# Sixteen of the 29 row sets gathered behind the lead latent block's merge, gathered behind the branches of all latent blocks instead

## The reference, cut to what matters

```
# branches: z and the two halves of the gMLP come from the same normalised input h
o  = rmsnorm(o, dn_norm) * silu(z)                     # z = h @ w_z
vg = rmsnorm(gelu(h @ w_vg), gm_norm)
gm = gelu(h @ w_u) * (w_s @ vg + b_s)                  # mixes positions inside a block of 128
# merge
merged = sigmoid(h @ w_ga) * (o @ w_a) + sigmoid(h @ w_gb) * (gm @ w_b)
x = x + gt1 * (merged @ w_out)
# PEER, for each token: 8 heads x 16 experts = 128 experts out of 16384, each a row of 2048
act = gelu(sum_d h2[d] * peer_u[expert, d]) * gate     # 128 dot products
y   = sum over the 128 experts of act * peer_v[expert] # 128 weighted additions
```

## Time and profile before

| what | value |
|---|---|
| median of 3 runs | 5527.45 us (5520.8 to 5527.68) |
| the profiled execution | 5512.66 us, its span 5510.9 us |
| busy, share of the span | PE 55%, PEld 38%, DVE 70%, ACT 9%, POOL 54% |
| DMA | 1866.24 MB, mean 339 GB/s |
| gathers (L320), as GpSimd's instructions | 640 of `peer_u` and 640 of `peer_v` |
| VectorE's uses of row sets | L367 x640, mean 2323 ns; L372 x635, mean 2357 ns |

### The profile page before, as it was taken

The page is one execution under the profiler, slowest core; times in us unless marked ns, Lnnn a source line. Parts: engine busy times, 40 slices in busy tenths (PEclk is TensorE's granted clock), DMA queues, the critical chain, the costliest instruction groups (busy, mean ns, idle before and its releaser), DMA issues. The chain is left out here.

```text
span 5510.9 us, 40820 instructions
## 1 busy us (share of the span) xinstructions
PE 3046.0 (55%) x15606; PEld 2074.5 (38%) x15606; DVE 3874.0 (70%) x4382; ACT 510.0 (9%) x834; POOL 2982.5 (54%) x1524
## 2 busy tenths in 40 slices
PE   5989978998999997979998893000000000000000
PEld 2786955448995447665554352000000000000000
DVE  2340017986675763267774689999999999999998
ACT  1521002422221000000000000000000000000000
POOL 0131002754654642104453522888888888888886
PEclk7999989999999998989999997555555555555555
DMA  9819878982226979959998854999999999999998
GB/s 398 347 54 342 322 293 322 395 359 96 88 85 265 388 277 375 383 215 379 420 420 361 328 209 180 422 420 422 422 421 420 420 419 420 421 409 422 422 422 363
DMA packets 269191, 1866.24 MB, mean 339 GB/s; under 512 B 31362, under 2 KB 35714, under 8 KB 48836
## 3 DMA queue, kind: packets, MB, share of 16 engines
q0 software_dynamic: 194560, 1409.51, 62.6%
q1 hardware_dynamic: 67812, 414.04, 19.4%
q10 hardware_dynamic: 6624, 40.07, 1.8%
HBM read 1844.56 MB, written 18.94 MB: 338 GB/s over the span
## 5 line engine op out<-in xcount | busy, mean ns | idle before, releaser
L220 PE MATMUL ps<-arena_sb 128*128 128x128 f32 (+2 forms) x8704 | 1872.9, 377 | 121.5 <-PEq L1641 31.6
L320 POOL DMA_INDIRECT arena_sb<-peer_v,arena_sb x640 | 1337.7, 2090 | 762.9 <-DVE arena_sb L372 475.4
L372 DVE SCALAR_TENSOR_TENSOR arena_sb<-arena_sb 128x2048 f32<-128x2048 f32 x635 | 1497.0, 2357 | 176.0 <-DMA arena_sb<-peer_v,arena_sb 99.4
L367 DVE CUSTOM_DVE_ANT_0 arena_sb<-arena_sb 128x2048 f32<-128x2048 f32 x640 | 1478.7, 2323 | 176.2 <-DMA arena_sb<-peer_u,arena_sb 174.5
L320 POOL DMA_INDIRECT arena_sb<-peer_u,arena_sb x640 | 1255.5, 1962 | 548.9 <-issue 275.5
L220 PEld LDWEIGHTS ps<-arena_sb 128*128 128x128 f32 x8704 | 1261.0, 195 | 748.1 <-issue 431.2
L266 POOL DMA_DIRECT2D arena_sb<-w_mod x64 | 34.9, 545 | 610.1 <-PE ps L227 487.6
L842 POOL TENSOR_TENSOR arena_sb<-arena_sb 128x1024 f32<-128x1024 f32 x60 | 197.9, 3307 | 202.7 <-ACT arena_sb L1100 166.9
L1502 PE MATMUL ps<-arena_sb 128*128 128x512 f32 x640 | 279.6, 599 | 30.9 <-PEq L1355 30.7
L1420 DVE TENSOR_TENSOR arena_sb<-ps,arena_sb 128x128 f32<-128x128 f32 (+1 forms) x96 | 35.2, 378 | 344.1 <-PE ps L220 343.0
L912 PE MATMUL ps<-arena_sb 128*128 128x64 f32 x1760 | 208.6, 277 | 0.0
(11 more groups left out here) (224 smaller groups left out, 2268.3 us busy)
## 6 DMA issues: line engine op xcount, KB each, us to landing
arena_sb<-w_mod POOLq DMA_DIRECT2D x64, 1024.0 KB, 8.8
arena_sb<-w_qkv SPq DMA_DIRECT2D x48, 1024.0 KB, 8.8
arena_sb<-w_ga SPq DMA_DIRECT2D x48, 1024.0 KB
arena_sb<-w_gb SPq DMA_DIRECT2D x48, 1024.0 KB
arena_sb<-w_out SPq DMA_DIRECT2D x48, 1024.0 KB, 7.5
arena_sb<-w_query SPq DMA_DIRECT2D x48, 1024.0 KB, 8.0
arena_sb<-w_mod SPq DMA_DIRECT2D x32, 1024.0 KB, 10.1
arena_sb<-w_a SPq DMA_DIRECT2D x48, 512.0 KB, 7.9
```

Of the source, the lines that this page charges most:

```text
L220: mm = pe.matmul(out, weights[:, k * P:(k + 1) * P], x[:, k, :], start=(k == 0), stop=(k == chunks - 1))
L320: nc.gpsimd.indirect_dma_start(slot, None, a["peer_v" if adds else "peer_u"], bass.IndirectOffsetOnAxis(ap=g.index[:, p:p + 1], axis=0)).t ...
L367: nc.vector.tensor_tensor_reduce(rows, rows, total, 1.0, 0.0, ALU.mult, ALU.add, g.dots[:, p:p + 1]).then_inc(t.rows_used, 1)
L372: nc.vector.scalar_tensor_tensor(out=total, in0=rows, scalar=g.weight[:, p:p + 1], in1=total, op0=ALU.mult, op1=ALU.add).then_inc(t.rows_u ...
```

## The change

It moves numbers in two lists. In the latent `branches` the eight z steps get 5, 4, 5, 4, 5, 4, 5, 4 row sets instead of 4 each, the run ahead of the norm of vg 40 instead of 34, and the first six u steps 5 instead of 4 (the seventh keeps 4, the eighth none): 4 + 6 + 6 = 16 more, 110 instead of 94. In the lead block's `merge` the steps get one set each for the first 13 and none for the last three, instead of two for 14 and one for the fifteenth: 13 instead of 29. From the end of that merge on, every set has the number, the slot and the place that it had.

```diff
@@ -1139,7 +1139,7 @@ def branches(nc, t, a, g):
     m0 = 3 * H
-    behind = take(t, [0] * (2 * H + 1) if ctx else [4] * H + [34] + [4] * (H - 1) + [0], 4)
+    behind = take(t, [0] * (2 * H + 1) if ctx else [5, 4] * (H // 2) + [40] + [5] * (H - 2) + [4, 0], 4)
     z_behind, vg_behind, u_behind = behind[0:H], behind[H], behind[H + 1:]
@@ -1348,7 +1348,7 @@ def merge(nc, t, a, g):
     sets = 1 if ctx else 2
-    behind = take(t, [0] * KD if ctx else [2] * (KD - 2) + [1, 0] if nb == 1 else [10] * (KD - 2) + [4, 0], 5)
+    behind = take(t, [0] * KD if ctx else [1] * (KD - 3) + [0, 0, 0] if nb == 1 else [10] * (KD - 2) + [4, 0], 5)
     m0 = 5 * H
```

## The result

The changed kernel takes 5536.73 us (median of 18 runs), the kernel before 5520.1 (18 runs): ratio 1.0026, interval 1.0019 to 1.0034. The medians differ by 16.6 us, the ratio says 14: slower, where 7.5 us faster was forecast. One run of the changed kernel, 5862.28 us at a granted clock of 0.704 instead of 0.774, was a slow one and is not in the ratio. The range, 5508 to 5533, missed the time by 3.7 us. It stood on the 5527.45 us of three runs; hung on the 5520.1 of eighteen it would have been 5501 to 5526, and the miss 11.

The account below looks back on a forecast made before the run. The lead merge was taken as bound by DMA, the latent branches as having TensorE full. Merge gain 28 us against branch cost 20.5 us gave -7.5, put on the median 5527.45: 5520 us, range 5508 to 5533.

Parts of the forecast that it names:

- VectorE leaves the z steps 5 us late: Latent branches, z steps: four more sets delay VectorE by 117.7 - 3.4 - 109 = 5 us, bounds 0 and 13.
- four full slots: Start of the z steps: the ring's slots are already full, credited as 4 x (3.27 - 2.43) = 3.4 us.
- The run ahead of the norm: Latent branches: six more sets at 3.27 us cost 19.6 us; with z's delay, TensorE waits 18.5 us ahead of `mix`.
- since weight loads run dry: Run ahead of the norm: weight loads stop while TensorE waits, so 1.5 us was taken off the delay.
- The lower clock: First `mix` and u steps after TensorE's new idle time: slower first records add 2 us, upper bound 3.
- The whole cost of the branches: Latent branches: TensorE's wait of 18.5 us plus 2 for the clock, 20.5 us; upper bound 31.
- The u steps: Latent branches: six more sets are covered by TensorE's own time, cost 0; steps stay at 17.06 us.
- the wait really goes: Lead merge: TensorE's 23.7 us of weight waits nearly vanish, 207.5 to 179.5 us; gain 28, at least 24, at most 31.
- one step and a half without a wait: Lead merge, near the fifteenth step: 144 TensorE records without a wait after one gather, taken as sign that waits go.
- The slower rival: Lead merge: loads issued 7.3 us before need still come late, 1 us a step stays; gain 7, sum +14, 5541; chance 0.08.
- The third: Z steps and run: gather issue limits four slots to 3.3 us a set; cost 30, gain 28, +2, 5529; chance 0.17.
- The 21 us ahead of the merge: Between the latent branches' end and the lead merge's start: TensorE's idle time of 21 us was taken as unchanged.

Follow-up runs that it names:

- z_only: Kernel before with only the four sets of the z steps moved there, merge keeping 25; ratio 1.0020 to the kernel before.
- vg_only: Kernel before with only the six sets of the run ahead of the norm moved there, merge keeping 23; ratio 1.0044 to the kernel before.
- wu_late: Changed kernel with the loads of u tiles 5 to 8 held until the run ahead of the norm is over; ratio 1.0028 to the kernel before.
- five_slots: Changed kernel with a ring of five slots instead of four in the z steps and the run; ratio 0.9984 to the kernel before.
- best3: Against the kernel before: five slots up to the norm, sets 36 in z, 38 in the run, 33 in u, 16 in the merge; ratio 0.9959.
- after_again: Changed kernel profiled once more, nothing altered; one run, 611.9 us from the first z matmul to the output projection's first.
- the second pair: Repeat profiles of the kernel before and the changed kernel, nothing altered; 592.1 and 611.9 us from first z matmul to the output projection's first.
- u_only: Kernel before with only the six sets of the u steps moved there, merge keeping 23; ratio 1.0005 to the kernel before.

## Why the prediction was wrong, point by point

- **The z steps.** The step that failed: "VectorE leaves the z steps 5 us late". The four sets cost 10.8 us (z_only). I had the ring's rate of 3.27 us a set, but credited four full slots that the kernel before has as well, so that credit cancels in a difference. And z had no room: the kernel before already waited for sets there (1.37 us at 1779.89) and used its 66 sets at 3.35 us each.
- **The run ahead of the norm.** Right at 19.6 us (vg_only: 20.0), and the path from VectorE's L1288 to `mix` was the right one. The 1.5 us that I took off "since weight loads run dry" were wrong in kind: in wu_late the run is no faster without the u tiles. TensorE's wait was 26.0 instead of 18.5.
- **The lower clock.** 2 us was too little: 2.6 in the first `mix` and 2.5 in the 32 records behind it (16.50 against 14.00), 5 in all. It does not grow with the wait: after 5.65 us (five_slots) the 32 records took 16.48, after 0.56 (best3) 16.88, after 27.5 (after_again) 15.73. The whole cost of the branches was 29.9 us (386.0 to 415.9 from S; 32.4 in the second pair), against 20.5; 31 was my upper bound.
- **The u steps.** Right: free, 17.06 us each.
- **The merge.** The step that failed: "the wait really goes". Its waits went from 23.7 to 10.4 us, not to 3, and moved from `w_gb` to `w_ga`; the gain was 20.9 us in one pair of profiles and 12.7 in the other, against 28 and a lower bound of 24. I had read the one step and a half without a wait as the rule. The same rows have another at 2096.78, where each step has two sets, so it was no sign of what fewer sets do. The slower rival had the mechanism, a load issued only 7.3 us before its use (7.1 in the trace) that lands later than that: 7.3 to 9.0 us at the changed kernel's waits. It cost 0.7 us a step instead of 1.
- **The rivals.** The third, the gather's turn-over, was right in its 30 us of cost, and I gave it 0.17. That the number fits is partly luck: its ten sets were to cost 33 us and moved the norm by 29.3, and its 2 us for the clock were 5. Its reason, issue between two uses, was not separated from the ring's depth. It missed the sum because it kept the merge's gain of 28. The outcome is that rival with half of the second's loss, a combination that no case of mine had.
- **Taken as given.** The 21 us ahead of the merge, which "stay as they are", did stay; but they were worth more than the change, and the trace of before had it: the last gathers land 16.5 us after TensorE's last matmul (2060.99 to 2077.51).

## What to carry to other kernels

DMA engines that are 95% busy don't say that the rate is the limit: look at what the same stretch moves against the best stretch of the trace (396 against 420 GB/s here), and count the slots. When work is moved between stages, an added set pays nearly its full price on the critical path of the new stage, while the old stage gives back only what its own next limit lets go; take the two as different prices. And look at when the last gather of a stage lands before giving work to its last steps.

## What the runs showed of the hardware

The merge behind the branches began 9.5 to 13.8 us after the last gather's issue had ended, and 4.5 to 5.3 us after its last packet; the output projection of u_only and vg_only 14.3 and 14.5 us after the last issue and 1.5 us after the last packet. Moving that gather forward moved the stage's end. A ring of 1 MiB gathers moved 341, 395 and 421 GB/s with three, four and five slots beside weight loads, with the DMA engines 0.85, 0.99 and 1.01 busy. After idle times of 5.65 to 27.6 us TensorE's first records ran at 0.80 instead of 0.38 to 0.49 us (in the changed kernel at a granted clock of 0.50, its lower level) and the 32 of 512 columns behind them took 15.49 to 16.75 instead of 14.00.
